# A streaming encoder step on one core: four orders changed and 24 identity products added

## The reference, cut to what matters

```python
def _trunk(x, ...):
    for layer in range(DEPTH):                      # DEPTH = 2
        h = _rmsnorm(x, norm_mix[layer])
        if layer % 2 == 0:
            mix, st = _even_mixer(h, w_in_even[j], ...)   # FoX (8 heads x 64) || mLSTM (4 heads x 128)
        else:
            mix, S = _odd_mixer(h, w_in_odd[j], ...)      # GLA (4 heads, dk=128, dv=256)
        x = x + mix @ w_out[layer]
        h = _rmsnorm(x, norm_ffn[layer])
        x = x + jnp.square(jax.nn.relu(h @ w_ff1[layer])) @ w_ff2[layer]
    return _rmsnorm(x, norm_final), ...
```

## Time and profile before

| | us |
|---|---|
| median of 3 runs | 2811.23 |
| lowest and highest of them | 2805.45, 2812.82 |
| profiled execution, its own time | 2798.42 |
| its span from first to last instruction | 2796.6 |

### The profile page before, as it was taken

The page is one execution under the profiler, slowest core; times in us unless marked ns, Lnnn a source line. Parts: engine busy times, 40 slices in busy tenths (PEclk is TensorE's granted clock), DMA queues, the critical chain, the costliest instruction groups (busy, mean ns, idle before and its releaser), DMA issues.

```text
span 2796.6 us, 44071 instructions
## 1 busy us (share of the span) xinstructions
PE 2719.7 (97%) x17332; PEld 2490.1 (89%) x17332; DVE 1628.5 (58%) x2162; ACT 1051.2 (38%) x1677; POOL 1351.9 (48%) x774
## 2 busy tenths in 40 slices
PE   8999999899999999999999999999999999999998
PEld 8999988687889889998899989998788999889997
DVE  6933247575576776667744410087367666776665
ACT  6552347463433333333324311356252333333233
POOL 4343455333456555555632231287355555565652
PEclk9999999999999999999999999999999999999999
DMA  6477330233474446544443131032575564355542
GB/s 213 149 261 256 137 124 2 83 119 138 139 268 166 173 142 221 213 154 170 164 150 122 46 124 54 1 129 69 196 211 188 206 220 160 141 187 206 204 173 82
DMA packets 207729, 430.65 MB, mean 154 GB/s; under 512 B 27285, under 2 KB 147441, under 8 KB 197108
## 3 DMA queue, kind: packets, MB, share of 16 engines
q1 hardware_dynamic: 197536, 389.68, 39.9%
q0 software_dynamic: 9216, 36.48, 3.5%
q10 hardware_dynamic: 852, 2.75, 0.3%
HBM read 357.89 MB, written 70.94 MB: 153 GB/s over the span
## 4 chain that ended last, share of the span: by engine, by line
PE 78%; DVE 9%; issue 4%; POOL 4%; ACT 3%; DMA 2%; POOLq 0%; PEld 0%; DVEq 0%; PEldq 0%; SPq 0%; ACTq 0%
PE ps L953 24%; PE ps L1031 22%; PE ps L575 8%; PE ps L636 6%; PE ps L585 4%; PE ps L2542 4%; PE ps L1113 4%; DVE units L3696 1%; DVE units L4155 1%; PE ps L2736 1%; DVE units L3698 1%; POOL units_r L712 1%; PE ps L3036 1%; DMA raw<-w_in_even 1%; POOL split L290 0%
## 5 line engine op out<-in xcount | busy, mean ns | idle before, releaser
L1326 POOL TENSOR_TENSOR split<-raw,split 128x1024 fp32r<-128x1024 f32 x218 | 568.2, 2617 | 491.5 <-ACT split L1164 465.6
L953 PE MATMUL ps<-units_r,split 128*128 128x288 f32 x5376 | 721.5, 296 | 14.2 <-POOL split L1326 5.4
L953 PEld LDWEIGHTS ps<-units_r,split 128*128 128x128 f32 x5376 | 718.6, 189 | 17.4 <-POOL split L1326 5.9
L1164 ACT ACTIVATE split<-raw 128x1024 fp32r<-128x1024 f32 x218 | 228.5, 1056 | 452.8 <-PE ps L953 178.5
L1441 DVE TENSOR_TENSOR units<-units,ps 128x512 f32<-128x512 f32 x434 | 285.5, 684 | 120.5 <-PE ps L1031 119.5
L575 PE MATMUL ps<-units_r,split 128*128 128x384 f32 x1872 | 328.8, 335 | 2.3 <-POOL split L290 1.5
L575 PEld LDWEIGHTS ps<-units_r,split 128*128 128x128 f32 x1872 | 324.4, 188 | 3.5 <-issue 1.6
L1031 PE MATMUL ps<-split,units_r 128*128 128x512 f32 x1344 | 309.2, 389 | 0.0
L1031 PEld LDWEIGHTS ps<-split,units_r 128*128 128x128 f32 x1344 | 252.3, 188 | 52.4
L1031 PE MATMUL ps<-split,spare_r 128*128 128x512 f32 x1008 | 235.6, 389 | 0.0
L1031 PEld LDWEIGHTS ps<-split,spare_r 128*128 128x128 f32 x1008 | 188.5, 188 | 38.6
(11 more groups left out here) (532 smaller groups left out, 4081.4 us busy)
## 6 DMA issues: line engine op xcount, KB each, us to landing
units_r<-operands SPq DMA_DIRECT2D x76, 2304.0 KB, 8.8
raw<-w_ff SPq DMA_DIRECT2D x128, 512.0 KB, 4.3
units_r<-operands SPq DMA_DIRECT2D x22, 1152.0 KB, 8.0
raw<-w_in_even SPq DMA_DIRECT2D x14, 1024.0 KB, 9.5
raw<-w_in_odd SPq DMA_DIRECT2D x12, 1024.0 KB, 5.3
operands<-units_r SPq DMA_DIRECT2D x10, 1152.0 KB, 5.6
operands<-units_r SPq DMA_DIRECT2D x22, 512.0 KB, 3.8
operands<-split SPq DMA_DIRECT2D x18, 512.0 KB, 3.8
```

Source lines behind the costliest of these rows:

```text
L953: last = pe.matmul(ps[:, bank + f, 0:HN], right_slot(base, slot, a)[:, COLS * k + P * f:COLS * k + P * (f + 1)], x[:, b, k, HN * g:HN * (g ...
L1164: act.activation(right_slot(base, slot, 0), src, ACT.Copy).then_inc(hi_ready, 1)
L1326: pool.tensor_tensor(right_slot(base, slot, 1), src, right_slot(base, slot, 0), ALU.subtract).then_inc(lo_ready, 1)
```

## The change

1. ScalarE, projection of layer 0: the evictions of `I_PROMPT` (prompt's input gate) and the copy of half g = 0 go first, then the high part of slot 3; the wait for `cb_back[2]` and `M_LOG`, `F_LOG` come after these, then the copy of half g = 1 and `I_SAMPLE`.
2. VectorE, projection of layer 0: `sum_low(5)`, the last sum's low part, stands ahead of `conv(6)`, the seventh convolution.
3. ScalarE, output projection of layer 0: `hi_of(base + 1)` comes after the high parts of tiles 0 and 1, not after tile 0 alone.
4. VectorE, MLP: `low(2, ...)` stands behind `squared(8)`, `s3` and the whole of `hidden_part(blk, 1, 1, ...)`.
5. TensorE: identity products at the samples' stages, 4 + 8 + 5 in the attention, 4 + 3 in the gated linear attention. There the wait for `l_free` is moved ahead of the waits for `l_qeb` and `l_sn`.

```diff
+        WARMING_FOXS = (4, 8, 5)
+        WARMING_GLAS = (4, 3)
...
                 mixed_high(act, layer, sources, n)
-                if n == 0 and not layer:
+                if n == 1 and not layer:
                     hi_of(act, base + 1, free=True)
...
                 hidden_part(blk, 0, 1, 9, 5, 5, ROW_BANKS)
-                low(2, half_of(left_ninth[:, 1, 0:2]), samples_of(plain, 0), half_of(left_ninth[:, 0, 0:2]))
                 squared(8)
                 dve.tensor_tensor(s3, p11, p21, ALU.subtract).then_inc(ff_sq, 1)
                 hidden_part(blk, 1, 1, 11, 3, 10, SUM_BANKS)
+                low(2, half_of(left_ninth[:, 1, 0:2]), samples_of(plain, 0), half_of(left_ninth[:, 0, 0:2]))
                 hidden_end(blk, 0)
...
             leave(pe, pe_stage)
+            keep_clock(pe, 7, WARMING_FOXS[0])
             enter(pe, S_FOXS)
...
             seq_keys(0)
             gate_rows()
+            keep_clock(pe, 7, WARMING_FOXS[1])
             seq_scores(0)
             seq_keys(1)
+            keep_clock(pe, 7, WARMING_FOXS[2])
...
             leave(pe, pe_stage)
+            pe.wait_ge(l_free, ring_taken[ring_place["level", PT, 7]])
+            keep_clock(pe, ring_place["level", PT, 7] % 4, WARMING_GLAS[0])
             pe.wait_ge(l_qeb, 1)
             pe.wait_ge(l_sn, 1 + 4 * PT)
-            pe.wait_ge(l_free, ring_taken[ring_place["level", PT, 7]])
             for h in range(GH):
                 gla_seq_out(h)
+            keep_clock(pe, ring_place["level", PT, 7] % 4, WARMING_GLAS[1])
             pe.wait_ge(l_keb, 1)
...
             sum_low(4)
+            sum_low(5)
             conv(6)
-            sum_low(5)
```

More of the change, by code:

```diff
@@ L3308, in _ @@
             act.wait_ge(gate_in, 64)
+            act.activation(I_PROMPT[:, 0:2 * GN].rearrange("p (g t) -> p g t", g=2), ps[0:4, 0:2, 0:GN], ACT.Identity,
+                           bias=gbias[0:4, 1:2])
+            act.activation(I_PROMPT[:, 2 * GN:SEQ], ps[0:4, 2, 0:256], ACT.Identity, bias=gbias[0:4, 1:2])
+            act.wait_ge(cb_back[0], 32)
+            act.wait_ge(cb_back[1], 32)
+            act.wait_ge(ff_h, 1)
+            act.activation(part_of(MO_OUT, 0, 0, 0), row_sums(0, SET_A), ACT.Copy).then_inc(ff_relu, 1)
+            summed_high(0, 3, quarters_of[0][0])
             act.wait_ge(cb_back[2], 64)
@@ L3311, in _ @@
             act.activation(as_groups(F_LOG), ps[32:40, 0:3, 0:GN], ACT.Identity, bias=gbias[32:40, 0:1]).then_inc(g_raw, 1)
-            act.activation(I_PROMPT[:, 0:2 * GN].rearrange("p (g t) -> p g t", g=2), ps[0:4, 0:2, 0:GN], ACT.Identity,
-                           bias=gbias[0:4, 1:2])
-            act.activation(I_PROMPT[:, 2 * GN:SEQ], ps[0:4, 2, 0:256], ACT.Identity, bias=gbias[0:4, 1:2])
+            act.wait_ge(ff_h, 2)
+            act.activation(part_of(MO_OUT, 0, 0, 1), row_sums(1, SET_A), ACT.Copy).then_inc(ff_relu, 1)
             act.activation(I_SAMPLE, ps[0:4, 2, 256:384], ACT.Identity, bias=gbias[0:4, 1:2]).then_inc(g_raw, 1)
-            act.wait_ge(cb_back[0], 32)
-            act.wait_ge(cb_back[1], 32)
-            for g in range(2):
-                act.wait_ge(ff_h, 1 + g)
-                act.activation(part_of(MO_OUT, 0, 0, g), row_sums(g, SET_A), ACT.Copy).then_inc(ff_relu, 1)
-                if g == 0:
-                    summed_high(0, 3, quarters_of[0][0])
             weight_summed(0, 2)
```

## The result

| | us |
|---|---|
| before, median of 6 executions | 2804.06 (2798.49 to 2812.82) |
| changed kernel, median of 6 | 2787.82 (2784.90 to 2791.65) |
| ratio, 95% interval | 0.995 (0.9938 to 0.9963) |
| profiled execution before, span, mean granted clock | 2798.42, 2796.6, 0.993 |
| profiled execution after, span, mean granted clock | 2788.57, 2786.8, 0.995 |

The time, 2787.8 us, is 15.4 under the forecast and under its range. The two profiled executions lie 9.8 us apart, where the sum said 8.0.

A forecast was written before the change was run, and what follows sets the result against it. TensorE, busy nearly all the time, was taken as the bound, so only its gaps and half clock could be won. -2.9 - 3.2 - 1.3 - 1.5 + 0.9 = -8.0 us gave 2803.2 us, range 2795 to 2811.

The forecast's parts named there:

- the sum: Whole kernel: five places together 8.0 us faster, 2790.4 for the profiled execution and 2803.2 for the median; chance 40%.
- second case: Whole kernel: half-clock stretches go elsewhere instead of away, so only 5.3 us faster, 2805.9 us; chance 25%.
- Gates: Layer 0's gates: ScalarE's copy comes by 144.4, so TensorE's whole 2.92 us gap goes; -2.9 us.
- Output projection: Layer 0's output projection: tile 1 ready before GpSimd begins, shorter gap and 1.3 us of half clock gone; -3.2 us.
- Attention: Samples' attention: identity products cost 0.1 us and remove the half clock at the first sequence; -1.3 us.
- MLP: First MLP block of each layer: VectorE's additions earlier, a transfer late next, 1.1 and 0.4 us won; -1.5 us.
- The case for slower: Twelve further MLP blocks: moved low part delays later ones 1.0 us a block, +12; net +4.0, 2815.2 us; chance 7%.
- Linear attention: Samples' gated linear attention: identity products fit idle time only in part, nothing counted for the clock; +0.9 us.
- The third: Whole kernel: more half clock goes than counted, -10.8 us, time 2800.4, down to 2797; chance 25%.
- its two spots: Half-clock stretches at 1953 (1.2 us) and in layer 1's first MLP block (1.55 us), which might also go.

The follow-up runs named there:

- 129 executions: Kernel before, unchanged, executed on the chips of the follow-up runs: mean 2801.2 us, from 2793.4 to 2809.6.
- the filled one: Changed kernel with identity products in more gaps (mLSTM end, value projection, ahead of linear attention): 2787.8 us; without the linear attention's own products, 2784.3 and 2786.0 us.
- 29 executions: Changed kernel, unedited, in its later executions after the first six: mean 2790.5 us, 10.8 under the kernel before.

## Why the prediction was wrong

**The anchor.** This is the step that failed most. The sum was made against the profiled execution, 2798.4, which gave 2790.4 for the changed kernel's; that was 2788.6. Then 12.8 us were carried over from the median of three. The mean of 129 executions is 2801.2, and two of those three, 2812.8 and 2811.2, are above the highest of them. The text's own warning, that a median of three may be off by 2 to 3 us, was too small: this one was off by 10.0. Of the 15.2 us between 2803.2 and the mean of the first six, 2788.0, that is two thirds. 2.8 more are the sum, 8.0 against 10.8, and 2.5 are the luck of those six.

**The clock's share.** The sum held 2.7 us of half clock (1.4 in the attention, 1.3 in the output projection); the runs show 5.3 by the estimate above, and the profile pair 5.0. In gaps, with the costs of the products taken off, it was near: 5.3, against 5.5 and 4.8. That nearness is in part luck: 2.3 us of the profile's gaps went at 768.8 and 2023.2, for which the sum had nothing, and the gaps of the two first MLP blocks grew by 0.6 where 1.5 less was forecast. The failed step is that one execution's stretches were priced as the kernel's. The text had the rule for it in its second case, but let it point one way only, to a smaller gain; it did not say that places with a stretch in other executions, and none in this one, were missing from the sum.

**Gates**, -2.9: the mechanism right (copy at 143.8, forecast 144.4, and no gap behind it). Size, 4.3 to 5.3: the gap, and a stretch of half clock behind it, 0.9 on average, that the earlier trace rows did not have.

**Output projection**, -3.2: right. 3.2 in the profile, 2.3 in the runs; a gap of 0.87 where 1 was said.

**Attention**, -1.3: right for this profile (1.4 of clock, 0.2 of products where 0.1 was charged), too small for the runs, about 2.3: 1.7 stretches on average in place of 1, one more behind in every profile without the products and in six of 14 with them, and the shorter gap 220 us later, for which its working had nothing.

**MLP**, -1.5: 0.8 to 1.5 in the runs, not clear of zero. `s3` and the late additions as said, and in the profile pair the last gap is ended by the transfer, at 1.54 and 1.53 us (forecast 1.4 and 2.1). Missed: the gaps before it (1.36 and 0.78 us in layer 0, 0.77 and 0.63 in layer 1), and that in other executions VectorE still ends the last one. Over the profiles the gain is in layer 0 alone, where 1.1 was forecast. The case for slower, 12 us in the loop, did not come.

**Linear attention**, +0.9: the products' own time, 1.04 us, is as counted. The profile lost more, by a half clock that lasts as long in most profiles without the products. Over the profiles the cost is 0.6; the runs do not show it in the changed kernel, and show 2.6 in the filled one. Open.

**The rivals.** The third, "more goes than I count", named -10.8 us, which is what 29 executions give. That is luck: of its two spots, the stretch at 1953 stayed, and the one in layer 1's first block went in this profile but is as frequent with the change as without. Its time of 2800.4 had the anchor's fault too.

## What to carry to other kernels

Before pricing a stretch of half clock, compare several executions of the kernel: where their time follows their mean clock, a thin place is worth the mean number of its stretches, and a gap with none behind it in the profile at hand can have some in the next. Tie the forecast to the profiled execution's own time and its clock, and let the range cover the distance to a median of few runs, instead of adding that distance. Identity products paid in idle time that ends with another engine's work. Between products that another engine paces one by one they made TensorE, in one profile, the one that is waited for.

## What the runs showed of the hardware

One kernel's executions spread over 16 us, nearly all of it with the clock, at 2.2 us for each 0.001 of its mean. A gap of 2.9 us had half clock behind it in four of seven profiles and none in three. With three thin places filled, no profile of four had half clock there, and the next thin place had one to two stretches. And 34 instructions more on TensorE's queue (the 17 products of the attention) went with a packet of instructions missing from a stretch 220 us later, and with a landing there 1.0 us shorter.
